# High parts of some weight panels moved 128 bytes on in their SBUF slots

## The chip, the cores and the metric

The kernel runs on one core of a Trainium2 chip. The metric is the device time of one execution in microseconds; three runs of the kernel before gave 839.09, 839.23 and 839.39 us (median 839.23).

## The reference

Two layers of a transformer on 256 tokens of width 1024, all in float32. Each layer has a mixer and a feed-forward part, both with a residual sum and a layer norm behind them:

```python
z = x @ w_in                                   # 1024 x 5904: latents, FoX q/k/v, DSA q/k/v, index, gates
o_mla = causal attention over keys/values made from a 128 wide latent (8 heads, 96 wide)
o_fox = causal attention with a cumulative log forget gate added to the scores (8 heads)
o_dsa = attention over the 64 keys picked by an index score (8 heads, shared key and value)
merged = sum_n sigmoid(gates_n + b_gate) * (o_n @ w_branch[n])
x = layernorm(ALPHA * x + merged @ w_out)
u = x @ w_up                                   # 1024 x 5632: gate and value halves
y = (gelu(conv3(u[..., :2816])) * u[..., 2816:]) @ w_down
x = layernorm(ALPHA * x + y)
```

## The kernel before, in words

**Products.** TensorE multiplies in a rounded float32 form. To keep the precision, every operand is split into a high part (rounded copy) and a low part (the rest), and a product is three matmuls, written by `product` (L670 to L674): `a_hi` with `b_hi` (L672), `a_hi` with `b_lo` (L673), `a_lo` with `b_hi` (L674). In each, `a` is the stationary operand (loaded into the array by LDWEIGHTS, 128 columns) and `b` the moving one. In a row's `ps<-X,Y` the first name is the moving operand and the second the stationary one. While one matmul streams its moving operand, the LDWEIGHTS of the next matmul reads that one's stationary tile.

**Panels.** The weights come in 72 panels a layer (`NP`), up to 2048 floats a partition. SP loads a panel into a slot of `raw` (six slots); ACT's `split_hi` (L1146) writes the high part into a slot of `w_hi` (four slots); DVE's `split_lo` (L1491) writes the low part into `w_lo`, which lies on the very addresses of `raw`. TensorE waits for `weights_lo` of the panel and frees it with `panel_used`. The order of all engines' work is written out by hand.

**Two ways to use a panel.** "By feature": the weight tile is stationary, the transposed activations are moving (FoX queries and keys, gates, branch panels, and 19 of the 22 up panels in `ffn_up`, L1012). "By token": the activations are stationary and the weights moving. By token go the two first panels (`A_AT`, 432 columns), the two panels of FoX values (`FV_AT`, 512 columns), the first three up panels (`up_by_token`, L1025, 256 columns), the out panels and the down panels (512 columns). FoX values are 24 matmuls a panel, 96 in the two layers. The up panels by token are done for token half 0 first (72 matmuls), then for half 1 (72), so 288 in the two layers; inside the third one of half 0 stand transposes of the second half of `x` (`turn_x`, L719), which wait for DVE's norm, and the first panel of half 1 waits for `x_lo_ready` before its fifth tile.

**Where the tiles lie.** The tensors lie one behind another in each partition, in the order of the code, so each address follows from the sizes. `raw` and `w_lo` start at byte 2,176, `w_hi` at 51,328, `xt_hi` and `xt_lo` (transposed `x`) at 92,480 and 100,672, `ot_hi` (attention outputs) at 116,032, `ot_hi_last` at 193,856, `mg_hi` at 173,184, `ht_hi` (hidden) at 133,248. Small unused tensors (`PADS`) set these. Taken modulo 256: `raw`, `w_lo`, `w_hi`, `mg` and `ht` have 128; `xt`, `ot` and `ot_last` have 64. `merged` has 192. Slots of 2048 floats are 8,192 bytes, which is 0 modulo 256. The first two panels of layer 0 are already moved by `FIRST_SHIFT` = 32 floats (128 bytes) in all three tensors (L437, L443, L449); in layer 1 they have places of their own (`early_hi` and `early_lo`, both 0 modulo 512), with tiles 1,728 bytes apart.

Of the kernel before, what the change touches and what calls it, by code (L numbers as in the profile page):

```python
# [19 lines left out]
F32R = mybir.dt.float32r  # L20
# [6 lines left out]
P = 128  # L27
# [30 lines left out]


PANEL = 2048  # L60

A_AT, FV_AT, FQ_AT, UQ_AT, FK_AT, KEYS_AT, IQ_AT, UKV_AT, SQ_AT = 0, 2, 4, 6, 7, 9, 10, 11, 12
GATE_AT = 14
# [2 lines left out]
UP_AT = OUT_AT + 4  # L66
# [1 line left out]
DOWN_K = [4, 3, 3, 3, 3, 3, 3]  # L68
NP = DOWN_AT + 2 * len(DOWN_K)
NGATED = 4  # L70
PADS = (48, 24, 112, 48, 208)
NHI, NLO = 4, 6
EARLY = (A_AT, A_AT + 1)
FIRST_SHIFT = 32
SKEWED = 4
UP_BY_TOKEN = 3

# [2 lines left out]
TAKEN = -3.3e38  # L80
# [57 lines left out]
def build_program(nc, x, positions, w_in, b_gate, b_forget, q_norm, kv_norm, w_uq, w_ukv, w_branch, w_out,  # L138
                  ln1_g, ln1_b, w_up, conv_w, conv_b, w_down, ln2_g, ln2_b, out):
    ctx = ExitStack()  # L140
    with ctx:
        def sb(name, shape, dt=F32):
            return ctx.enter_context(nc.sbuf_tensor(name, shape, dt))
# [123 lines left out]
        def slot_of(l, p, n):  # L267

            return n + p - A_AT if is_early(l, p) else turn_of(l, p) % n
# [13 lines left out]
        with ExitStack() as over:  # L283
            raw = over.enter_context(nc.sbuf_tensor("raw", [P, NLO, PANEL], F32))
        w_lo = sb("w_lo", [P, NLO, PANEL], F32R)
        w_hi = sb("w_hi", [P, NHI, PANEL], F32R)
        x_tok = sb("x_tok", [P, NT, DM])
        sb("beside_x", [P, PADS[0]])
        xt_hi = sb("xt_hi", [P, KD, T], F32R)
# [14 lines left out]
        eps = sb("eps", [P, 2])  # L304
        sb("beside_outputs", [P, PADS[1]])
        with ExitStack() as over:
# [14 lines left out]
        with ExitStack() as att:  # L321
            sa = sized(att)
            z1 = sa("z1", [P, NT, ZW])
            gates_early = sa("gates_early", [P, SLOTS // 2, T])
            with ExitStack() as over:
                so = sized(over)
                rel_first = so("rel_first", [P, 4, T])
                rel_second = so("rel_second", [P, 4, 2 * T])
            gates_late = sa("gates_late", [P, SLOTS // 2, T])
            with ExitStack() as over:  # L330
                so = sized(over)
                merged = so("merged", [P, KD, T])
                gated = so("gated", [P, NGATED, T])
            fq_t = sa("fq_t", [P, 4, T])
            fk_t = sa("fk_t", [P, 4, T])
            fv = sa("fv", [P, NT, H * HD])
            sa("beside_merged", [P, PADS[2]])
            with ExitStack() as over:
                so = sized(over)
                mg_hi = so("mg_hi", [P, KD, T], F32R)  # L340
                mg_lo = so("mg_lo", [P, KD, T], F32R)
            qm_t = sa("qm_t", [P, H, T])
            km_t = sa("km_t", [P, H, T])
            v_tok = sa("v_tok", [P, NT, H * HD])
            sa("beside_last", [P, PADS[3]])
            with ExitStack() as over:
                so = sized(over)
                ot_hi_last = so("ot_hi_last", [P, 4, T], F32R)
                ot_lo_last = so("ot_lo_last", [P, 4, T], F32R)
            decay = sa("decay", [P, H, T])  # L350
            decay_first = sa("decay_first", [P, H, P])
            sq_t = sa("sq_t", [P, 4, T])
            sk_t = sa("sk_t", [P, T])
            with ExitStack() as over:
                so = sized(over)
                pts_odd = so("pts_odd", [P, 2, 3 * P])
            ik_t = sa("ik_t", [P, T])
            iq_t = sa("iq_t", [P, 2, T])
            rsum = sa("rsum", [P, 2, 2, NT])
            rinv = sa("rinv", [P, 2, 2, NT])  # L360
            least = sa("least", [P, 2, 2, NT])
            small = sa("small", [P, 16])
            fx = sa("fx", [P, NT, H])
            fe = sa("fe", [P, NT, H])
            fl = sa("fl", [P, NT, H])
            cum = sa("cum", [P, NT, H])
            with ExitStack() as lat:
                sl = sized(lat)
                sl("beside_latents", [P, 24])
                c_hi = sl("c_hi", [P, 3, T], F32R)  # L370
                c_lo = sl("c_lo", [P, 3, T], F32R)
                with ExitStack() as over:
                    so = sized(over)
                    c_f = so("c_f", [P, 3, T])
                    cn = so("cn", [P, NT, QR + KVR])
                rot = sl("rot", [P, 4, NT, H, HALF])
                q_rope = sl("q_rope", [P, NT, H * ROPE])
                krot = sl("krot", [P, 4, NT, HALF])
                kr = sl("kr", [P, NT, ROPE])
            with ExitStack() as heads:  # L380
                sh = sized(heads)
                prob = sh("prob", [P, 2, 2, 3 * P])
                pts_even = sh("pts_even", [P, 2, 3 * P])
                ix = sh("ix", [P, 3 * P])
                ixw = sh("ixw", [P, 3 * P])
                top8 = sh("top8", [P, 8])
                selm = sh("selm", [P, 3 * P])

        with ExitStack() as ffn:
            sf = sized(ffn)  # L390
            sf("beside_hidden", [P, PADS[4]])
            ht_hi = sf("ht_hi", [P, FT, T], F32R)
# [30 lines left out]
        SPAN = (slice(0, P), slice(P, 3 * P))  # L423
# [9 lines left out]
        def panel_raw(l, p):  # L433

            if is_early(l, p):
                return early_raw[:, p - A_AT, :]
            return raw[:, slot_of(l, p, NLO), FIRST_SHIFT if p in EARLY else 0:]  # L437

        def panel_lo(l, p):

            if is_early(l, p):
                return early_lo[:, p - A_AT, :]
            return w_lo[:, slot_of(l, p, NLO), FIRST_SHIFT if p in EARLY else 0:]  # L443

        def panel_hi(l, p):

            if is_early(l, p):
                return early_hi[:, p - A_AT, :]
            return w_hi[:, slot_of(l, p, NHI), FIRST_SHIFT if p in EARLY else 0:]  # L449

        def turned(i):

# [159 lines left out]
        def panel_extents(p):  # L612
# [9 lines left out]
            if p >= DOWN_AT:  # L622
                return [(P, slice(0, 512 * DOWN_K[(p - DOWN_AT) % len(DOWN_K)]))]
            return [(P, slice(0, PANEL))]

# [43 lines left out]
        def _(pe):  # L669
# [387 lines left out]
            for l in range(DEPTH):  # L1057
# [71 lines left out]
                for c in range(2):  # L1129
                    for g in range(ng if c == 0 else ng - SKEWED):  # L1130
                        k0, nk = sum(DOWN_K[:g]), DOWN_K[g]
# [3 lines left out]
                        for t, ins in by_token(l, DOWN_AT + ng * c + g, k0, nk, 512, (ht_hi, ht_lo), B_R[c],  # L1135
                                               g == 0, g == ng - 1):
                            if g == ng - 1 and t == 0:
                                ins.then_inc(s_residual_product, 1)
                        ins.then_inc(s_panel_used, 1)
                one_token_first(l, [(NP - ng + g, 1, sum(DOWN_K[:g]), DOWN_K[g], False, g == ng - 1)  # L1140
                                    for g in range(ng - SKEWED, ng)], (ht_hi, ht_lo), SKEWED - 1 if l < DEPTH - 1 else None)

# [347 lines left out]
        def _(dve):  # L1490
# [106 lines left out]
            def take_eight(l, n):  # L1597

                t = n // (TOPK // 8)
                if n % (TOPK // 8) == 0:  # L1600
                    dve.wait_ge(s_index_masked, at("index_masked", l, t + 1))
                dve.drain()
                dve.max(top8[:], ixw[:, SPAN[t]])
                dve.drain()
                dve.match_replace(ixw[:, SPAN[t]], top8[:], ixw[:, SPAN[t]], TAKEN)

            def selection(l):

# [410 lines left out]
```

## Time and profile before

| | us |
|---|---|
| median of three runs | 839.23 |
| the profiled execution, whole | 840.46 |
| its span, first to last instruction | 838.7 |
| TensorE matmuls busy | 826.2 (99% of the span) |
| VectorE busy | 605.2 (72%) |
| ScalarE busy | 464.1 (55%) |

The profile is one execution of the program. Matmuls are pipelined: one lasts longer than the distance to the start of the next, and their ends are modelled, so what a matmul costs is read from the distance between starts, and its recorded duration is only a sign of it.

### The profile page before, as it was taken

What the parts mean: (1) busy time and instruction counts of PE and PEld (TensorE: products, weight loads), DVE (VectorE), ACT (ScalarE), POOL (GpSimd) and SP (SyncE); (2) the same over time, 40 slices, a digit from 0 to 9 for tenths busy, and PEclk for the clock granted to TensorE, in tenths of its full rate; (3) what the DMA queues carried; (4) which work ended last, traced back from release to release, by engine and by line L of the source; (5) the groups of instructions that cost most, each with busy time, mean ns of one, the idle gap of its engine ahead of it and who ended that gap; (6) DMA issues with size and microseconds to landing.
All of it is one profiled execution on the core that took longest, in us unless ns stands there. A gap on an engine that the chain in (4) does not pass through costs nothing.

```text
span 838.7 us, 15687 instructions
## 1 busy us (share of the span) xinstructions
PE 826.2 (99%) x6326; PEld 770.9 (92%) x6326; DVE 605.2 (72%) x1076; ACT 464.1 (55%) x701; POOL 113.8 (14%) x133
## 2 busy tenths in 40 slices
PE   7999999999999999999999999999999999999996
PEld 6899999999899999988889998998998999999885
DVE  5675788987786877765676568888797687777554
ACT  5675866663456655543447576756545475555440
POOL 1503910006300000000000067000180000000000
PEclk9999999999999999999999999999999999999999
DMA  9959643344579766475847694443467767764731
GB/s 307 240 131 280 192 137 117 136 152 151 165 189 240 197 193 184 160 244 175 267 114 190 127 333 118 145 131 122 151 185 198 190 190 195 200 189 151 250 115 50
DMA packets 190265, 150.98 MB, mean 180 GB/s; under 512 B 32653, under 2 KB 164337, under 8 KB 189937
## 3 DMA queue, kind: packets, MB, share of 16 engines
q1 hardware_dynamic: 181120, 143.09, 57.9%
q10 hardware_dynamic: 9072, 6.90, 3.0%
q8 instruction: 50, 0.82, 0.4%
q14 instruction: 23, 0.18, 0.1%
HBM read 148.63 MB, written 1.06 MB: 178 GB/s over the span
## 4 chain that ended last, share of the span: by engine, by line
PE 92%; DMA 2%; DVE 2%; POOLq 1%; SPq 1%; ACT 1%; ACTq 1%; POOL 1%; issue 0%; DVEq 0%
PE ps L672 28%; PE ps L674 27%; PE ps L673 27%; PE ps L955 3%; PE ps L986 2%; PE ps L967 2%; POOLq L1989 1%; DMA decay<-decay_rows 1%; DMA raw<-w_in 1%; PE ps L730 1%; DVE w_lo L1499 1%; ACTq L1203 0%; ACT w_hi L1154 0%; PE ps L1052 0%; POOL rel_first L1986 0%
## 5 line engine op out<-in xcount | busy, mean ns | idle before, releaser
L1499 DVE TENSOR_TENSOR w_lo<-raw,w_hi 128x2048 fp32r<-128x2048 f32 (+2 forms) x140 | 303.2, 2167 | 111.5 <-ACT w_hi L1154 111.4
L672 PE MATMUL ps<-xt_hi,w_hi 128*128 128x256 f32 x1232 | 344.9, 280 | 0.0
L673 PE MATMUL ps<-xt_lo,w_hi 128*128 128x256 f32 x1232 | 340.6, 276 | 0.0
L674 PE MATMUL ps<-xt_hi,w_lo 128*128 128x256 f32 x1232 | 340.5, 276 | 0.0
L1154 ACT ACTIVATE w_hi<-raw 128x2048 fp32r<-128x2048 f32 (+3 forms) x142 | 253.0, 1786 | 77.9 <-PE ps L674 71.0
L672 PEld LDWEIGHTS ps<-xt_hi,w_hi 128*128 128x128 f32 x1232 | 231.3, 188 | 3.3 <-issue 2.0
L673 PEld LDWEIGHTS ps<-xt_lo,w_hi 128*128 128x128 f32 x1232 | 231.7, 188 | 0.0
L674 PEld LDWEIGHTS ps<-xt_hi,w_lo 128*128 128x128 f32 x1232 | 231.3, 188 | 0.0
L672 PE MATMUL ps<-w_hi,ht_hi 128*128 128x512 f32 x176 | 68.6, 390 | 0.0
L674 PE MATMUL ps<-w_hi,ht_lo 128*128 128x512 f32 x176 | 68.5, 389 | 0.0
L673 PE MATMUL ps<-w_lo,ht_hi 128*128 128x512 f32 x176 | 68.5, 389 | 0.0
L1275 ACT ACTIVATE cv<-ps,vec_t 128x256 f32<-128x256 f32 x44 | 20.8, 474 | 81.4 <-PE ps L674 77.8
L1999 POOL TENSOR_TENSOR merged<-merged,gated 128x256 f32<-128x256 f32 x32 | 40.2, 1282 | 177.3 <-DVE gated L1681 177.3
L1238 ACT ACTIVATE prob<-prob,least 128x128 f32<-128x128 f32 x96 | 42.8, 448 | 17.3 <-DVE least L1639 17.3
L672 PE MATMUL ps<-w_hi,xt_hi 128*128 128x256 f32 (+2 forms) x144 | 46.4, 322 | 0.9 <-DVE xt_lo L1506 0.7
L674 PE MATMUL ps<-w_hi,xt_lo 128*128 128x256 f32 (+2 forms) x144 | 45.1, 313 | 0.0
L673 PE MATMUL ps<-w_lo,xt_hi 128*128 128x256 f32 (+2 forms) x144 | 45.0, 312 | 0.0
L1971 POOL COPY km_t<-km_t 32x1792 f32<-32x1792 f32 x2 | 3.3, 1673 | 294.2 <-ACT km_t L1231 294.2
L1729 DVE SCALAR_TENSOR_TENSOR cv<-ps,vec_t,cv 128x255 f32<-128x255 f32 x44 | 21.2, 483 | 30.2 <-ACT cv L1275 29.9
L674 PEld LDWEIGHTS ps<-w_hi,ht_lo 128*128 128x128 f32 x176 | 33.0, 188 | 6.9
L672 PEld LDWEIGHTS ps<-w_hi,ht_hi 128*128 128x128 f32 x176 | 33.0, 188 | 6.8
L673 PEld LDWEIGHTS ps<-w_lo,ht_hi 128*128 128x128 f32 x176 | 33.0, 188 | 6.7
(252 smaller groups left out, 1276.1 us busy)
## 6 DMA issues: line engine op xcount, KB each, us to landing
raw<-ffn_w_up SPq DMA_DIRECT2D x88, 512.0 KB, 5.2
raw<-w_in SPq DMA_DIRECT2D x84, 512.0 KB, 5.5
raw<-ffn_w_down SPq DMA_DIRECT2D x32, 512.0 KB, 4.0
raw<-w_branch SPq DMA_DIRECT2D x24, 512.0 KB, 4.4
raw<-w_out SPq DMA_DIRECT2D x16, 512.0 KB, 4.6
raw<-ffn_w_down SPq DMA_DIRECT2D x24, 256.0 KB, 3.0
decay<-decay_rows ACTq DMA_DIRECT2D x2, 1024.0 KB, 8.6
ln_g<-ln_g ACTq DMA_DIRECT2D x4, 512.0 KB, 3.5
```

The costliest lines, as they stand in the source:

```text
L672: pe.matmul(dst, a_hi, b_hi, start=first, stop=False)
L673: pe.matmul(dst, a_hi, b_lo, start=False, stop=False)
L674: return pe.matmul(dst, a_lo, b_hi, start=False, stop=last)
L955: ins = pe.matmul(ps[:, B_S[a], SPAN[t]], q[:, P * t:P * t + P], k[:, 0:P * (t + 1)], start=True, stop=True)
L967: ins = pe.transpose(ps[:, B_PT[a], P * c:P * c + P], prob[:, i % 2, a, P * c:P * c + P], ident[:])
L986: ins = pe.matmul(dst[HD * a:HD * a + HD, P * c:T], v, turned(i)[:, a, cols], start=c == 0, stop=c == 1)
L1154: ins = act.activation(panel_hi(l, p)[0:n, cols], panel_raw(l, p)[0:n, cols], ACT.Copy)
L1238: ins = act.activation(p, p, ACT.Exp, scale=-1.0, bias=least[:, i % 2, a, t:t + 1], accum_out=rsum[:, i % 2, a, t:t + 1])
L1275: act.activation(cv[:, buf, :], ps[:, B_UP[f % len(B_UP)], 0:T], ACT.Copy, scale=column(vec_t, V_CW + 2 * FT, f)).then_inc(s_conv_first_ta ...
L1499: ins = dve.tensor_tensor(low, panel_raw(l, p)[0:n, cols], panel_hi(l, p)[0:n, cols].bitcast(F32), ALU.subtract)
L1729: dve.scalar_tensor_tensor(cv[:, buf, 1:T], ps[:, B_UP[f % len(B_UP)], 0:T - 1], column(vec_t, V_CW + FT, f), cv[:, buf, 1:T], ALU.mult, A ...
L1999: pool.tensor_tensor(merged[:, u % KD, :], merged[:, u % KD, :], gated[:, u % NGATED, :], ALU.add).then_inc(s_merged_added, 1)
```

## The change

The high parts of seven panels (the two first ones, as before, and now also the two of FoX values and the three up panels by token) begin 32 floats (128 bytes) into their slot of `w_hi`. Their raw and low parts stay where they were, except for the two first ones, which were moved already. For this the slots of `w_hi` become 64 floats (256 bytes) longer, `SLOT` = 2112. To find the room, a pad in front of `mg_hi` shrinks from 112 to 48 floats, and the small tile `top8` (top eight index scores) takes the place of another pad instead of room of its own.

```diff
+SLOT = PANEL + 64
-PADS = (48, 24, 112, 48, 208)
+PADS = (48, 24, 48, 48, 208)
+SHIFTED = (A_AT, A_AT + 1, FV_AT, FV_AT + 1, UP_AT, UP_AT + 1, UP_AT + 2)
-        w_hi = sb("w_hi", [P, NHI, PANEL], F32R)
+        w_hi = sb("w_hi", [P, NHI, SLOT], F32R)
-            sa("beside_last", [P, PADS[3]])
+            top8 = sa("top8", [P, PADS[3]])
-                top8 = sh("top8", [P, 8])
-            return w_hi[:, slot_of(l, p, NHI), FIRST_SHIFT if p in EARLY else 0:]
+            at0 = FIRST_SHIFT if p in SHIFTED else 0
+            return w_hi[:, slot_of(l, p, NHI), at0:at0 + PANEL]
-                dve.max(top8[:], ixw[:, SPAN[t]])
+                dve.max(top8[:, 0:8], ixw[:, SPAN[t]])
-                dve.match_replace(ixw[:, SPAN[t]], top8[:], ixw[:, SPAN[t]], TAKEN)
+                dve.match_replace(ixw[:, SPAN[t]], top8[:, 0:8], ixw[:, SPAN[t]], TAKEN)
```

No instruction is added or removed. Everything that lies behind `w_hi` moves by 1,024 bytes, what lies behind the shortened pad (`mg_hi` and on, within the attention part) by 768, and `selm` by 736.

## Rows read from the trace of the kernel before

**Rows 1.** The page, part 1: busy us (share of the span) xinstructions.
```profile
PE 826.2 (99%) x6326; PEld 770.9 (92%) x6326; DVE 605.2 (72%) x1076; ACT 464.1 (55%) x701; POOL 113.8 (14%) x133
```

**Rows 2.** The page, part 4: shares of the chain that ended last.
```profile
PE 92%; DMA 2%; DVE 2%; POOLq 1%; SPq 1%; ACT 1%; ACTq 1%; POOL 1%; issue 0%; DVEq 0%
```

**Rows 3.** Timeline (start us, duration us, instruction) of PE, a feature-wise up panel, layer 0.
```profile
278.54 0.28 PE L672 MATMUL ps<-xt_hi,w_hi 128*128 128x256 f32 x1
...
283.98 0.28 PE L672 MATMUL ps<-xt_hi,w_hi 128*128 128x256 f32 x1
```

**Rows 4.** Timeline of PE, up panels by token, layer 0, first half of tokens.
```profile
237.06 0.28 PE L672 MATMUL ps<-w_hi,xt_hi 128*128 128x256 f32 x1
...
244.01 0.28 PE L674 MATMUL ps<-w_hi,xt_lo 128*128 128x256 f32 x1
```

**Rows 5.** Timeline of PE, a down panel of three tiles, layer 0.
```profile
373.98 0.39 PE L673 MATMUL ps<-w_lo,ht_hi 128*128 128x512 f32 x1
...
378.06 0.39 PE L673 MATMUL ps<-w_lo,ht_hi 128*128 128x512 f32 x1
```

**Rows 6.** Timeline of PE, FoX value panels of layer 1, second half of tokens.
```profile
436.81 0.39 PE L672 MATMUL ps<-w_hi,xt_hi 128*128 128x512 f32 x1
...
442.08 0.40 PE L674 MATMUL ps<-w_hi,xt_lo 128*128 128x512 f32 x1
```

**Rows 7.** Groups by line, same stretch: xcount | busy us, mean ns.
```profile
L672 PE MATMUL ps<-w_hi,xt_hi 128*128 128x512 f32 x8 | 3.2, 394 | 0.0
L674 PE MATMUL ps<-w_hi,xt_lo 128*128 128x512 f32 x8 | 3.1, 393 | 0.0
L673 PE MATMUL ps<-w_lo,xt_hi 128*128 128x512 f32 x8 | 3.1, 388 | 0.0
```

**Rows 8.** Timeline of PE, first feature-wise panel (FoX queries) of layer 0.
```profile
31.94 0.28 PE L673 MATMUL ps<-xt_lo,w_hi 128*128 128x256 f32 x1
...
37.59 0.28 PE L673 MATMUL ps<-xt_lo,w_hi 128*128 128x256 f32 x1
```

**Rows 9.** Line L674: duration ns min/median/max, first and last start us.
```profile
L674 PE MATMUL ps<-xt_hi,w_lo x1232: 276/276/286, 32.1 to 771.2; 128*128 128x256 f32 x176
...
L674 PE MATMUL ps<-ot_hi_last,w_lo x64: 281/281/281, 202.9 to 625.1; 128*128 128x256 f32 x64
```

**Rows 10.** Timeline of PE, the two first panels of layer 1 (432 columns).
```profile
433.31 0.35 PE L672 MATMUL ps<-early_hi,xt_hi 128*128 128x432 f32 x1
...
433.90 0.35 PE L672 MATMUL ps<-early_hi,xt_hi 128*128 128x432 f32 x1
...
435.65 0.35 PE L672 MATMUL ps<-early_hi,xt_hi 128*128 128x432 f32 x1
...
436.24 0.35 PE L672 MATMUL ps<-early_hi,xt_hi 128*128 128x432 f32 x1
```

**Rows 11.** Timeline of PE around its two waits in the up panels by token.
```profile
244.32 0.66 PE L730 MATMUL ps<-ident,x_tok 128*128 128x128 f32 x4
...
248.25 0.39 PE L672 MATMUL ps<-w_hi,xt_hi 128*128 128x256 f32 x1
```

**Rows 12.** Timeline of DVE, what those two waits wait for.
```profile
243.51 0.75 DVE L1719 SCALAR_TENSOR_TENSOR x_tok<-res,rdev,ln_b 128x512 f32<-128x512 f32 x1
...
247.50 0.69 DVE L1506 TENSOR_TENSOR xt_lo<-ps,xt_hi 128x512 fp32r<-128x512 f32 x1 [1.15 <-ACT xt_hi L1161]
```

**Rows 13.** Timeline of DVE: the normed latents that PE takes after FoX values, layer 1.
```profile
441.20 0.94 DVE L1544 TENSOR_SCALAR cn<-z,small 128x192 f32<-128x192 f32 x4
```

**Rows 14.** Lines L1744, L1686, L1255, L1286: duration ns min/median/max, first and last start.
```profile
L1744 DVE TENSOR_TENSOR ht_lo<-hf,ht_hi x44: 417/419/429, 260.7 to 775.9; 128x256 fp32r<-128x256 f32 x44
...
L1686 DVE SCALAR_TENSOR_TENSOR mg_lo<-merged,mg_hi x16: 411/681/986, 209.2 to 629.4; 128x256 fp32r<-128x256 f32 x16
...
L1255 ACT ACTIVATE mg_hi<-merged x16: 400/419/420, 206.4 to 628.9; 128x256 fp32r<-128x256 f32 x16
...
L1286 ACT ACTIVATE ht_hi<-hf x44: 401/407/419, 260.2 to 775.5; 128x256 fp32r<-128x256 f32 x44
```

## The prediction

> **What bounds the kernel.** I read the page's busy shares first: TensorE is busy for 826.2 of 838.7 us [rows 1]. The chain of waits confirms it, with 92% of the span on PE [rows 2]. So time can only move where matmuls start closer together or further apart, or where TensorE waits. No instruction changes, so everything hangs on addresses, and I read the timeline for the distance between matmul starts, against the addresses that the front part lists.
>
> Call D the moving operand's address minus that of the stationary tile loaded beside it, modulo 256. I pick 256 because all the pads differ within it; what speaks for that period stands below.
>
> - D = 0 (down panels: `w` and `ht` both at 128): from 373.98 to 378.06 us are 18 matmuls of 512 columns, 226.7 ns each [rows 5].
> - D = 64 (up panels by token, `w` at 128 moving, `xt` at 64 stationary): the 60 matmuls from 237.06 to 244.01 make 59 distances of 117.8 ns [rows 4]. FoX values have the same D: 24 matmuls, 23 distances over 5.27 us, 229.1 ns each [rows 6]. By line, the two kinds that stream `w_hi` last 394 and 393 ns, the one that streams `w_lo` 388 [rows 7].
> - D = 192 (feature-wise panels, `xt` moving, `w` stationary): 48 matmuls from 278.54 to 283.98, 113.3 ns each [rows 3]. But the same D also has a dear price: the first FoX query panel of layer 0 takes 117.7 ns for each of its 48 (31.94 to 37.59) [rows 8]. By duration, 276 ns is the median of the 1232 feature-wise ones and 281 that of all 64 on `ot_hi_last`, which have D = 192 as well [rows 9].
>
> So a matmul of 256 columns has two prices, 113.3 and 117.8, 4.5 ns apart. At D = 64 I see only the dear one; at D = 192 mostly the cheap one, and in some runs of panels the dear one throughout. What picks the price at D = 192 no row tells me.
>
> **The change part by part.**
>
> *The shift.* `w_hi` of the seven panels goes from 128 to 0 modulo 256. For FoX values and the three up panels a matmul that streams `w_hi` (L672 and L674, two in three) then has D = 0 - 64 = 192; the one that streams `w_lo` (L673) keeps 64. Up panels: if L672 and L674 go to the cheap price, each gains 4.5 ns. The lower end is 0 (D = 192 at its dear price costs 117.7, what they cost now, so no row has a loss here); the upper end is that all three kinds get it, as each LDWEIGHTS shadows a neighbour. I take the two kinds in three: the row of FoX values already has the third apart from the others.
>
> Which of them are on the path? TensorE waits twice in these panels. At 244.32 it starts transposes 0.31 us after the last matmul before them (244.01) [rows 4, 11], where 0.12 is the usual distance; DVE's norm, 243.51 to 244.26, ends just before [rows 12]. DVE began that chain from the out product, so the 60 matmuls before it gain nothing: TensorE waits longer instead. The 12 behind it are on the path, since the next transposes follow them and ACT and DVE follow those. The next 12 are hidden again: the matmul behind them starts at 248.25, just after the end of DVE's `xt_lo` (247.50 to 248.19) [rows 11, 12]. The last 60 are on the path: nothing but TensorE stands between 248.25 and the feature-wise panels. So 72 of 144 a layer, 144 in both, of which 96 stream `w_hi`: 96 x 4.5 ns = 0.43 us (0 to 144 x 4.5 = 0.65).
>
> FoX values: 96 matmuls. Down panels show what 512 columns cost without the loss, 226.7 [rows 5], against 229.1 [rows 6]: 96 x 2.4 = 0.23 us, between 0 and, from the durations of 394 and 393 against 388, 64 x 5.5 = 0.35. In layer 1 TensorE goes from them to the transposes of the latents, at 442.08 + 0.23 = 442.31 [rows 6], and DVE has those ready at 441.20 + 0.94 = 442.14 [rows 13]. The cover is 0.17 us and the last 24 matmuls gain 24 x 2.4 = 0.06, so nothing is late next. In layer 0 the transposes wait for a copy that itself follows TensorE. All 96 count.
>
> *The splits.* ACT then writes `w_hi` at 128 bytes from its source modulo 256, and DVE reads `raw` and `w_hi` at such a distance; 10 panels. The nearest rows: DVE on `merged` (192) and `mg_hi` (128) has a minimum of 411 ns, on `hf` and `ht_hi` (both 128) 417; ACT has minima of 400 and 401 with and without an offset of 64 [rows 14]. The medians of 681 and 419 are in the stretch where GpSimd adds `merged`. I take 0. Were it 411 against 417 either way, 10 panels of eight times the length would move by 10 x 8 x 6 ns = 0.5 us of DVE time, which stands beside TensorE.
>
> *Longer slots, moved tensors.* A slot step of 8,448 bytes is 33 x 256: odd slots get 256 bytes more, all D stay. 1,024 and 768 are multiples of 256 too. Is 256 the whole period? The two first panels of layer 1 differ by 256 modulo 512. Their third tile (D = 64 in one, 320 modulo 512 in the other) takes 433.31 to 433.90 and 435.65 to 436.24: 0.59 us for three matmuls both times [rows 10]. I take 0. `selm` (736 bytes) and `top8` only meet DVE; 0.
>
> **The sum.** 0.43 + 0.23 = 0.66 us, so 840.46 - 0.66 = 839.80 for the profiled execution, which was 1.23 us above the median; on the scale of the runs 839.23 - 0.66 = **838.6 us**, 0.08% less. With the ends: 839.2 to 838.2.
>
> Differences under 0.2% (1.7 us) I call no change; this is about what a measurement of this kernel can tell.
>
> **A rule that speaks against it.** What the rows show first: matmuls of the same shape, back to back, differ by 4.5 ns with the addresses [rows 3, 4]. The Trainium skill (SBUF — State Buffer, "Who interferes with whom") says that TensorE has two independent read ports, one for the moving operand and one for LDWEIGHTS, and never waits on anyone. By that rule D has no price, and the sum would be 0. The trace doesn't agree with it fully, though it doesn't prove that the addresses are the cause.
>
> **Rivals.**
>
> 1. *Nothing moves.* The by-token order costs 117.8 for another reason (the order of reads, the `w_lo` matmul that holds its neighbours at the dear price), as D = 192 also has 117.7 [rows 8]. For it: a price seems to persist over whole panels. Against: FoX values, where just the kinds on `w_hi` are long [rows 7]. 839.2 us.
> 2. *More panels turn cheap.* The price may be handed on from one panel to the next. The queries and first keys of layer 0 (144 matmuls) run right behind FoX values; freed, they give 144 x 4.5 = 0.65 us more: 837.9. The branch matmuls on `ot_hi_last` (64 of each kind, 192 in both layers [rows 9]) would give 192 x 4.5 = 0.86 us more: 837.1. Against the second part: what stands before them keeps its D. With both, and 0.2 for `w_lo` on top, 836.9.
> 3. *Slower: the other up panels turn dear.* The 19 feature-wise up panels follow the moved ones, and they have the cheap price [rows 3]. If the new alternation of 192 and 64 hands them the dear price, 912 matmuls a layer cost 4.5 ns more, 4.1 us: 843 us with one layer, 847 with both. It decides at the first panel behind the up panels by token; from about 520 such matmuls (521 x 4.5 = 1.7 + 0.66 us) it is over the bound. Against: transposes with a gap lie between, and behind gaps this D nearly always ends cheap.
> 4. *Slower: 512 is the period.* Then odd slots have a D of their own; half of 3696 feature-wise matmuls dear is 1848 x 4.5 = 8.3 us: 847. Against it rows 10.
>
> **How the numbers follow.** Forecast as priced (838.2 to 839.0): 0.52. Rival 1: 0.18. Rival 2: 0.18, of which 0.12 under 837.6 (its second part included). Rival 3: 0.08. Rival 4: 0.04. Faster by over 0.2% (below 837.6): 0.12 from rival 2 and 0.04 for a gain on `w_lo` and on waits together with the first part of rival 2: 0.16. Slower: 0.12. Within: 0.72. The range of 8 in 10 is 837.2 to 839.9: it leaves out the far end of rival 2 and rivals 3 and 4.
>
> **What would show it.** In the trace after: L672 and L674 of the up panels by token last 276 instead of 280 ns, L673 stays; distances there average (2 x 113.3 + 117.8) / 3 = 114.8. In FoX values L672 and L674 last 388, distances 227. The wait before 244.3 grows by 60 x 3.0 = 0.2 us. Feature-wise panels and splits keep their durations, in odd slots too. The forecast fails if the by-token distances stay at 117.8, if a panel elsewhere changes its price, or if `split_lo` of the ten panels leaves 2.29 us.

## The result and the profile after

The changed kernel took 843.42 us (median of 20 executions, 839.49 to 847.72), the kernel before beside it 839.20 (838.78 to 839.88, one execution of 1389.82 set aside). The ratio is 1.0040, with an interval of 1.0030 to 1.0051: slower by 0.4%, where no change was forecast. A median hides the shape: six executions lie at 839.5 to 840.6, thirteen at 843.2 to 844.6 and one at 847.7. That is three levels, some 4 us apart. The profiled execution is one of the middle level (843.45 us, span 841.7). In the changed kernel `product` has the lines L674, L675 and L676.

The page, busy shares, and the shares of the chain [rows 1, 2]:
```profile
PE 829.5 (99%) x6326; PEld 774.1 (92%) x6326; DVE 605.5 (72%) x1076; ACT 464.4 (55%) x701; POOL 112.9 (13%) x133
```
```profile
PE 91%; POOL 3%; DVE 2%; issue 1%; DMA 1%; SPq 1%; ACT 1%; POOLq 0%; DVEq 0%
```
Only TensorE has moved, by 3.3 us in as many instructions: no engine has taken its place as the bound.

Timeline of PE in layer 0, the 18 feature-wise up panels behind the four transposes (start us, duration us, instruction), first and last of 864 matmuls, and the first down matmul:
```profile
261.03 0.60 PE L1054 MATMUL ps<-ident,u_tok 128*128 128x128 f32 x4
261.39 0.36 PE L674 MATMUL ps<-xt_hi,w_hi 128*128 128x256 f32 x1
261.59 0.28 PE L675 MATMUL ps<-xt_lo,w_hi 128*128 128x256 f32 x1
...
363.11 0.28 PE L676 MATMUL ps<-xt_hi,w_lo 128*128 128x256 f32 x1
363.23 0.39 PE L674 MATMUL ps<-w_hi,ht_hi 128*128 128x512 f32 x1
```
The same block in layer 1:
```profile
675.89 0.60 PE L1054 MATMUL ps<-ident,u_tok 128*128 128x128 f32 x4
676.24 0.37 PE L674 MATMUL ps<-xt_hi,w_hi 128*128 128x256 f32 x1
676.45 0.28 PE L675 MATMUL ps<-xt_lo,w_hi 128*128 128x256 f32 x1
...
774.15 0.28 PE L676 MATMUL ps<-xt_hi,w_lo 128*128 128x256 f32 x1
774.26 0.39 PE L674 MATMUL ps<-w_hi,ht_hi 128*128 128x512 f32 x1
```
Layer 0: 363.11 - 261.39 = 101.72 us over 863 distances, 117.9 ns each. Layer 1: 97.91, 113.5 each, as before [rows 3]. The same panels, at addresses that the change did not move against one another, cost 3.8 us more in one layer than in the other. Two such layers, one or none would make the three levels; of the changed kernel only the middle one was profiled. No single row shows it, each matmul lasts 0.28 us in both: one has to divide a stretch by its count.

Up by token, layer 0, first and last of 60 [rows 4]; the second half of the FoX values of layer 1, first and last of 24 [rows 6]; and the first panel of FoX queries of layer 0, first and last of 48 [rows 8]:
```profile
236.13 0.28 PE L674 MATMUL ps<-w_hi,xt_hi 128*128 128x256 f32 x1
...
243.09 0.28 PE L676 MATMUL ps<-w_hi,xt_lo 128*128 128x256 f32 x1
...
439.94 0.39 PE L674 MATMUL ps<-w_hi,xt_hi 128*128 128x512 f32 x1
...
445.25 0.40 PE L676 MATMUL ps<-w_hi,xt_lo 128*128 128x512 f32 x1
```
```profile
31.57 0.37 PE L674 MATMUL ps<-xt_hi,w_hi 128*128 128x256 f32 x1
...
36.99 0.28 PE L676 MATMUL ps<-xt_hi,w_lo 128*128 128x256 f32 x1
```
By token: 6.96 us over 59, 118.0 ns, no gain. FoX values: 5.31 over 23, 230.9, where 229.1 stood: dearer. FoX queries: 5.42 over 47, 115.3 with the long first distance of 0.20 us in it; behind that one the distance went from 117.8 to 113.4 in all 96 matmuls of the queries (0.4 us saved). In layer 1 the same panels went the other way.

Where the 3.0 us of span came from, from distances times counts: TensorE reaches the up panels by token 0.93 us earlier (236.13 against 237.06, of which the queries are 0.41 and the branch panels 0.37); then the first feature-wise panel of layer 0 costs 48 x 4.3 = 0.2 and the block 864 x 4.4 = 3.8. The down product starts 363.23 - 360.14 = 3.1 us later, and layer 1, where small terms of both signs cancel (queries and one gate panel +0.6, keys and branch -0.6), keeps it.

### The profile page after: what moved, and what is told of

It reads as the page before. It is cut to its first block, busy times and chain, and to the rows that moved or that the text cites. A ratio compares the mean times of both kernels' runs of the same rounds, so it can differ in the third digit from the quotient of the medians.

```text
span 841.7 us, 15687 instructions
## 1 busy us (share of the span) xinstructions
PE 829.5 (99%) x6326; PEld 774.1 (92%) x6326; DVE 605.5 (72%) x1076; ACT 464.4 (55%) x701; POOL 112.9 (13%) x133
## 4 chain that ended last, share of the span: by engine, by line
PE 91%; POOL 3%; DVE 2%; issue 1%; DMA 1%; SPq 1%; ACT 1%; POOLq 0%; DVEq 0%
PE ps L674 28%; PE ps L676 27%; PE ps L675 27%; POOL merged L2001 3%; PE ps L957 3%; PE ps L969 2%; PE ps L988 2%; DVE w_lo L1501 1%; DMA raw<-w_in 1%; ACT w_hi L1156 1%; PE ps L732 1%; PE ps L919 0%; PE ps L1054 0%; SPq L636 0%; DVE x_tok L1721 0%
## 5 line engine op out<-in xcount | busy, mean ns | idle before, releaser
L1501 DVE TENSOR_TENSOR w_lo<-raw,w_hi 128x2048 fp32r<-128x2048 f32 (+2 forms) x140 | 303.1, 2167 | 112.2 <-ACT w_hi L1156 111.8
L674 PE MATMUL ps<-xt_hi,w_hi 128*128 128x256 f32 x1232 | 346.4, 281 | 0.0
L675 PE MATMUL ps<-xt_lo,w_hi 128*128 128x256 f32 x1232 | 342.1, 278 | 0.0
L676 PE MATMUL ps<-xt_hi,w_lo 128*128 128x256 f32 x1232 | 342.1, 278 | 0.0
L1156 ACT ACTIVATE w_hi<-raw 128x2048 fp32r<-128x2048 f32 (+3 forms) x142 | 252.7, 1784 | 77.8 <-PE ps L676 71.3
L674 PEld LDWEIGHTS ps<-xt_hi,w_hi 128*128 128x128 f32 x1232 | 232.6, 189 | 3.3 <-issue 2.0
L675 PEld LDWEIGHTS ps<-xt_lo,w_hi 128*128 128x128 f32 x1232 | 231.6, 188 | 0.0
L676 PEld LDWEIGHTS ps<-xt_hi,w_lo 128*128 128x128 f32 x1232 | 231.5, 188 | 0.0
L674 PE MATMUL ps<-w_hi,ht_hi 128*128 128x512 f32 x176 | 68.6, 390 | 0.0
L676 PE MATMUL ps<-w_hi,ht_lo 128*128 128x512 f32 x176 | 68.5, 389 | 0.0
L675 PE MATMUL ps<-w_lo,ht_hi 128*128 128x512 f32 x176 | 68.5, 389 | 0.0
L674 PE MATMUL ps<-w_hi,xt_hi 128*128 128x256 f32 (+2 forms) x144 | 46.5, 323 | 0.4 <-DVE w_lo L1501 0.4
L675 PE MATMUL ps<-w_lo,xt_hi 128*128 128x256 f32 (+2 forms) x144 | 45.2, 314 | 0.0
L676 PE MATMUL ps<-w_hi,xt_lo 128*128 128x256 f32 (+2 forms) x144 | 45.2, 314 | 0.0
L676 PEld LDWEIGHTS ps<-w_hi,ht_lo 128*128 128x128 f32 x176 | 33.0, 188 | 6.9
L674 PEld LDWEIGHTS ps<-w_hi,ht_hi 128*128 128x128 f32 x176 | 33.0, 188 | 6.8
L675 PEld LDWEIGHTS ps<-w_lo,ht_hi 128*128 128x128 f32 x176 | 33.0, 188 | 6.8
```

The source lines that it names most:

```text
L674: pe.matmul(dst, a_hi, b_hi, start=first, stop=False)
L675: pe.matmul(dst, a_hi, b_lo, start=False, stop=False)
L676: return pe.matmul(dst, a_lo, b_hi, start=False, stop=last)
L1156: ins = act.activation(panel_hi(l, p)[0:n, cols], panel_raw(l, p)[0:n, cols], ACT.Copy)
L1501: ins = dve.tensor_tensor(low, panel_raw(l, p)[0:n, cols], panel_hi(l, p)[0:n, cols].bitcast(F32), ALU.subtract)
```

## The experiments

Below, "the block" is the 864 matmuls of feature-wise up panels 4 to 21 of a layer, "the first panel" is panel 3 ahead of it, "cheap" is about 113.3 ns and "dear" about 117.8 ns between starts. Experiments whose ratios are given together ran beside the same executions of the kernel before. A mean distance leaves out the pauses at waits; where it is taken over a whole stretch from first to last start, the first long distance is in it.

### Which part of the change does it

The kernel before took 839.62 us beside these. `e1_slots` has the longer slots and the moved small tensors, but shifts only the two first panels; `e1_fv` also FoX values; `e1_up` also the up panels, without FoX values.
```diff
-SHIFTED = (A_AT, A_AT + 1, FV_AT, FV_AT + 1, UP_AT, UP_AT + 1, UP_AT + 2)
+SHIFTED = (A_AT, A_AT + 1)                                  # e1_slots
+SHIFTED = (A_AT, A_AT + 1, FV_AT, FV_AT + 1)                # e1_fv
+SHIFTED = (A_AT, A_AT + 1, UP_AT, UP_AT + 1, UP_AT + 2)     # e1_up
```


> Longer slots, the shorter pad and the moved top8, but no further panel shifted. Theory 1 and 3: 839.2 us, all up panels at 113.3 ns. Theory 2 (odd slots or moved tensors): levels of 839.5, 843.5 and 847.7 as after.

> Only the two FoX value panels are shifted. Theory 1: the up panels stay at 113.3 ns; the queries of layer 0 may be cheap and FoX values cost 231 instead of 229 ns (both as in the profile after), so 838.5 to 839.5 us. Theory 2: 839.5 to 847.7, several levels. Theory 3: 843.5 and 847.7 appear here.

> Only the three up panels by token are shifted (the FoX value panels lie as before). Theory 1 (the by-token up panels hand their price on to the 19 up panels behind them: the alternation of D = 192 and 64 ends in the dear phase): some executions at about 839.5, 843.5 and 847.7 us, as after; in the profile a layer's 912 matmuls at 117.8 ns in at least one execution. Theory 2 (the longer slots or moved tensors do it): the same times, but then also without any shift. Theory 3 (the FoX value shift does it): 839 us throughout.

Measured: slots 839.77 us (1.0004, 0.9995 to 1.0012), FoX values 840.04 (1.0005, 0.9996 to 1.0014), up panels 842.69 (1.0038, 1.0019 to 1.0057). The first two have eleven executions each, and none at a level: the highest are 841.68 and 842.00, and nothing recorded says why these two are 2 us above their median. The third has the levels: six of twelve at 839.6 to 841.5, four at 843.9 to 844.7, two at 847.2 and 848.2. So the loss belongs to the shift of the up panels by token. In its profile the block is cheap in layer 0 and dear in layer 1, the mirror of the changed kernel:
```profile
672.45 0.60 PE L1054 MATMUL ps<-ident,u_tok 128*128 128x128 f32 x4
672.81 0.36 PE L674 MATMUL ps<-xt_hi,w_hi 128*128 128x256 f32 x1
673.01 0.28 PE L675 MATMUL ps<-xt_lo,w_hi 128*128 128x256 f32 x1
...
774.53 0.28 PE L676 MATMUL ps<-xt_hi,w_lo 128*128 128x256 f32 x1
```
In layer 1 the block takes 774.53 - 672.81 = 101.72 us over 863 distances, 117.9 ns each. The FoX value matmuls of `e1_fv` take 231.1 ns in both layers: their shift costs by itself.

These runs also show something of the up panels by token, which the prediction took as dear by their address. In layer 1 of `e1_slots`, where these panels are not shifted, the last 60 of them (token half 1) run cheap:
```profile
659.28 0.38 PE L674 MATMUL ps<-w_hi,xt_hi 128*128 128x256 f32 x1
...
666.07 0.28 PE L676 MATMUL ps<-w_hi,xt_lo 128*128 128x256 f32 x1
```
6.79 us over 59, 115.1 ns; without the first long distance 113.3. Layer 0 of `e1_fv` does the same, and the other layer of each stays at 117.8. So an address difference of 64 has both prices too.

Two more divide the up panels: `e2_first` shifts panels 0 and 1 of the three, `e2_last` panel 2, the last before the feature-wise ones.
```diff
+SHIFTED = (A_AT, A_AT + 1, UP_AT, UP_AT + 1)                # e2_first
+SHIFTED = (A_AT, A_AT + 1, UP_AT + 2)                       # e2_last
```


> The first and second up panel are shifted, the third is not. Theory 1: 839.6 us throughout, f = 3 at 113.6 ns in both layers. Rival 1b: levels of 839.6, 843.8 and 848. If the third panel carries on what the second leaves, a mixture.

> Of the up panels only the third, the last one by token before the feature-wise ones, is shifted. Theory 1 (the last by-token panel hands its price on): levels of 839.6, 843.8 and 848 us as in the run with all three, and the first feature-wise up panel (f = 3) at 117.8 ns in both layers. Rival 1b (the first shifted panel starts it): 839.6 us, f = 3 at 113.6.

Measured, beside 839.48 us: 839.93 us (1.0006, 0.9997 to 1.0014) and 839.90 (1.0004, 0.9995 to 1.0012), no execution of eleven each above 841.0. Each theory expected levels from one of the two, and neither has them. With panels 0 and 1 the first panel is cheap in both layers; with panel 2 it is dear in layer 1, cheap in layer 0; with all three shifted it is dear in the eight profiled layers where eight transposes stand ahead of it (two layers each of the changed kernel, `e1_up` and the two kernels with breaks below), and cheap in both layers of `e3_nobreak` below, where twelve do. So the last shifted panel can turn the next one; a dear block I have seen only with all three shifted.

### Is it the address difference?

Five variants of the kernel before, with nothing but pads changed, so that `xt` lies elsewhere modulo 256.
```diff
-PADS = (48, 24, 112, 48, 208)
+PADS = (64, 8, 112, 48, 208)       # e1_xt128: tiles at 128
+PADS = (16, 56, 112, 48, 208)      # e2_xt192: at 192
+PADS = (32, 40, 112, 48, 208)      # e2_xt0: at 0
+PADS = (56, 16, 112, 48, 208)      # e3_xt96: at 96
+PADS = (40, 32, 112, 48, 208)      # e3_xt32: at 32
```


> The kernel before, with xt_hi and xt_lo 64 bytes further on (128 modulo 256): D = 0 for feature-wise and by-token panels of 1024 wide inputs. Theory A (the conflict depends on D and D = 0 is free, as the down panels show at 226.7): all of these at 113.3 ns, by token too, no second price: about 144 x 4.5 + 96 x 2.4 + 340 x 4.5 ns = 2.4 us less, 836.8 us. Theory B (at 256 columns both streams meet in one bank for the whole matmul when D = 0): 117.8 ns or more for all 4300 matmuls, 858 us or more. Theory C (addresses have no price, only the order and phase of instructions): 839.2 us.

> The kernel before with xt_hi and xt_lo at 192 modulo 256: D becomes 64 for feature-wise and 192 for all three kinds by token. If D alone sets the price: by token 113.3 to 117.8 ns, feature-wise 117.8 for some 3000 matmuls, 13 us more, 852 us. If the order matters and not D: 839.2.

> The kernel before with xt at 0 modulo 256: D = 128 in both orders. The 432 column panels of the kernel before have about 196.5 ns at D = 128 against 192 to 193 at 0, so I expect a price between 113.3 and 119.9; at 117.8 it is 852 us, at 113.3 without a second price 837.

> The kernel before with its stationary tiles of turned states moved to byte 96 of the period of 256 (difference 224 feature-wise, 32 by token; was 192 and 64). Theory (the price goes by the difference, and 0 gives 120.0, 192 gives 113.3 or 117.8): 224 lies between them, 113.3 to 120.0 ns for the 256-column matmuls feature-wise, so 839 to 856 us; a steady cheap price would give 839, a steady one of 117.8 some 850. Rival (only steps of 64 bytes count, 224 behaves as 192 and 32 as 0): 839 to 845 us.

> The same with the tiles at byte 32 (difference 160 feature-wise, 96 by token). Theory: between the prices of 128 and 192, that is 113.3 to 118.7 ns feature-wise, 839 to 856 us. Rival (steps of 64 bytes count, 160 behaves as 128 and 96 as 64): as the tiles at byte 0, about 856 us.

Measured (mean distance in ns between starts; D is the prediction's, moving minus stationary modulo 256; where two values stand, layer 0 and 1, or two groups of panels):

| `xt` at | D by feature | 256 columns | D by token | 256 columns | 512 columns | us, ratio |
|---|---|---|---|---|---|---|
| 64 (before) | 192 | 113.4, some 117.8 | 64 | 117.8 | 229.1, 229.5 | 839.28 to 839.62 |
| 192 | 64 | 117.8, some 113.4 | 192 | 117.3, 115.7 | 233.3, 233.1 | 852.94, 1.0161 |
| 32 | 160 | 117.3, 118.8 | 96 | 119.8 | 233.3 | 854.66, 1.0184 |
| 96 | 224 | 118.3 | 32 | 117.3, 116.9 | 233.1, 233.3 | 856.32, 1.0205 |
| 0 | 128 | 118.7 | 128 | 120.0 | 232.2, 233.2 | 858.07, 1.0223 |
| 128 | 0 | 120.0 | 0 | 119.8 | 226.7, 228.9 | 862.05, 1.0266 |

Addresses alone are worth 22 us here, and the place of before is the best of the six. The down panels, whose tiles did not move, kept 226.7 to 226.9 ns throughout. For 256 columns the difference 0 is among the dearest (119.8 to 120.0, with 128), for 512 it is the cheapest; 192 has the cheap price for 256 and is among the dear ones for 512 (all but 0 and 64 lie at 232.2 to 233.5). Of the expectations, those hold that priced by the difference (theory B of `e1_xt128`, 852 us for `e2_xt192`, 118.7 ns feature-wise in `e2_xt0`, a price between its neighbours for 224 and, but for the groups at 118.8, for 160); those fall that took 0 as free, the addresses as without a price, or only steps of 64 as counting.

The difference doesn't settle everything: at 0, with all three kinds alike, the FoX values of layer 1 keep 228.9. And by token at 192, again with all three kinds alike, the first 60 of `e2_xt192` stay dear in both layers; layer 0:
```profile
239.45 0.28 PE L672 MATMUL ps<-w_hi,xt_hi 128*128 128x256 f32 x1
...
246.40 0.28 PE L674 MATMUL ps<-w_hi,xt_lo 128*128 128x256 f32 x1
```
6.95 us over 59, 117.8 ns. Of the last 60, those of layer 0 have 117.8 and those of layer 1 113.6. Groups by line, `e1_xt128`, layer 0, feature-wise (xcount | busy us, mean ns):
```profile
L674 PE MATMUL ps<-xt_hi,w_lo 128*128 128x256 f32 x209 | 59.1, 283 | 0.0
L672 PE MATMUL ps<-xt_hi,w_hi 128*128 128x256 f32 x209 | 59.1, 283 | 0.0
L674 PEld LDWEIGHTS ps<-xt_hi,w_lo 128*128 128x128 f32 x209 | 40.1, 192 | 0.0
L672 PEld LDWEIGHTS ps<-xt_hi,w_hi 128*128 128x128 f32 x209 | 40.1, 192 | 0.0
L673 PEld LDWEIGHTS ps<-xt_lo,w_hi 128*128 128x128 f32 x209 | 40.1, 192 | 0.0
```
Here each of these LDWEIGHTS lasts 192 ns. The same groups of the changed kernel, in its dear block and in its cheap one:
```profile
L674 PEld LDWEIGHTS ps<-xt_hi,w_hi 128*128 128x128 f32 x283 | 54.3, 192 | 0.0
L675 PEld LDWEIGHTS ps<-xt_lo,w_hi 128*128 128x128 f32 x284 | 53.3, 188 | 0.0
L676 PEld LDWEIGHTS ps<-xt_hi,w_lo 128*128 128x128 f32 x284 | 53.3, 188 | 0.0
...
L674 PEld LDWEIGHTS ps<-xt_hi,w_hi 128*128 128x128 f32 x283 | 53.1, 188 | 0.0
L675 PEld LDWEIGHTS ps<-xt_lo,w_hi 128*128 128x128 f32 x283 | 53.1, 188 | 0.0
L676 PEld LDWEIGHTS ps<-xt_hi,w_lo 128*128 128x128 f32 x282 | 52.9, 188 | 0.0
```
In a dear stretch at D = 192 exactly one load of three is long, the same line for 864 matmuls; in a cheap one none is. At this difference the state of a stretch can be read from that row. By token at a difference of 64 it can't: the kernel before has 117.8 ns there with all loads at 187 to 188.

### Is the state set at the entry and held?

`e3_nobreak` moves the last four transposes ahead of the first panel, so that all 19 panels run without a break. `e3_reset` adds breaks to the changed kernel ahead of panels 5, 6, 7 and 8, `e4_reset1` one ahead of panel 5.
```diff
+                turn_up(l, 2)                                # e3_nobreak
                 ffn_up(l, 3)
-                turn_up(l, 2)
...
+                if f in (5, 6, 7, 8):                        # e3_reset; e4_reset1: f == 5
+                    for _ in range(2):
+                        pe.transpose(ps[:, B_UP[f % len(B_UP)], 0:P], ident[:], ident[:])
```


> The changed kernel with the last turn of the hidden state moved ahead of the first feature-wise up panel, so that the transposes no longer stand between that panel and the 18 behind it. Theory (price set at the entry and held): all 19 panels of a layer have one price, 912 matmuls at either 113.3 or 117.8 ns, so the levels lie at about 839.5, 843.6 and 847.7 us, with no mixed case of a first panel that is dear and a block that is cheap; and as the first panel was dear in every profile with a shifted panel, 847.7 in most. Rival (what makes the block dear is the entry at the second panel alone, behind the four transposes): the break is gone and with it the cause, and all executions lie at 839.5 to 840.5 us.

> The changed kernel with two extra identity transposes ahead of each of the feature-wise up panels 5 to 8 of both layers (16 in all, output never read). Theory (the price of a stretch of panels is set where the matmuls begin again after other work, and held until the next such place): a block that enters at 117.8 ns gets four more entries and turns to 113.3 at one of them, so dear blocks last at most some 48 to 240 matmuls, 1.1 us instead of 3.9; executions at 843 us and above vanish or become rare, and the median falls to 840 to 842 us, the extra transposes costing up to 16 x 0.11 us and up to 8 x 0.1 us of re-entry. Rival (the layer's price is settled by something else than the entry: addresses, the buffer in turn, the partner load): the blocks stay at 117.8, the median is 844 to 846 us and the three levels of the changed kernel stay, 1 to 2 us higher.

> The changed kernel with two extra identity transposes ahead of the feature-wise up panel 5 alone, in both layers (their output is never read). With four such breaks (ahead of panels 5 to 8) the executions lay together at 842.0 to 843.0 us. Theory (a panel block takes its price at the entry and holds it; a block that came in dear gets another entry and turns cheap): the levels of the changed kernel at 843 to 845 us vanish, and with two breaks in place of eight the median is 840.0 to 840.8 us. Rival (an entry is a draw with no regard to what went before, so one more entry changes nothing but where the draw is made): the levels stay with the same shares, median 843 to 844 us, and the profile shows blocks of 816 matmuls at 117.8 ns.

`e3_nobreak` (before: 839.28): seven executions at 838.7 to 839.4 and five at 843.3 to 843.8, median 839.38, ratio 1.0021 (1.0006 to 1.0036). None is at 847, and the share that the theory expected was wrong: most executions had no dear layer. The times can't tell a dear layer of 912 from one of 864, and only one execution, of the lower level, was profiled. That profile has all 912 cheap in both layers (end of the stretch of layer 1):
```profile
666.74 0.37 PE L674 MATMUL ps<-xt_hi,w_hi 128*128 128x256 f32 x1
...
770.09 0.28 PE L676 MATMUL ps<-xt_hi,w_lo 128*128 128x256 f32 x1
```
103.35 us over 911, 113.4 each. The first panel, dear in every profile of the changed kernel's order, is cheap here. The rival (the cause is the second entry alone) falls as well, since five executions are still on the upper level.

`e3_reset`: 842.65 us (five executions, 841.97 to 843.0), ratio 1.0039 (1.0027 to 1.0051). None of the five shows the cost of a dear block, but the breaks eat the gain and the median misses the 840 to 842 us of the theory: in both layers the prices by panel are dear, cheap, cheap, dear, cheap, and the remaining 672 cheap. The 96 dear ones a layer cost 2 x 96 x 4.5 = 0.9 us, so by the times the eight breaks cost 842.65 - 839.5 - 0.9 = 2.3, some 0.28 each (an estimate). The trace gives 0.26: 257 ns from the last start of a panel to the first of the next in place of 114, and 47 distances of 115.7 in place of 113.3 behind it. Panel 6 shows that a break is no repair. It is entered from a cheap panel and is dear in both layers (47 distances of 119.5):
```profile
272.85 0.28 PE L676 MATMUL ps<-xt_hi,w_lo 128*128 128x256 f32 x1
272.97 0.38 PE L1021 MATMUL ps<-ident 128*128 128x128 f32 x2
273.10 0.36 PE L674 MATMUL ps<-xt_hi,w_hi 128*128 128x256 f32 x1
273.30 0.28 PE L675 MATMUL ps<-xt_lo,w_hi 128*128 128x256 f32 x1
```

`e4_reset1` (before: 839.09): three executions at 840.0 to 841.0, three at 843.6 to 844.4, median 842.31, ratio 1.0043 (1.0028 to 1.0057). The theory falls: one more entry doesn't remove the levels. The rival is right in that, but its blocks of 816 dear matmuls were not seen, since the one profile is of the lower level, 840.00 us, and has both blocks cheap behind the break. There layer 1 enters dear twice (panels 3 and 4) and leaves it at the break:
```profile
672.35 0.36 PE L674 MATMUL ps<-xt_hi,w_hi 128*128 128x256 f32 x1
672.55 0.28 PE L675 MATMUL ps<-xt_lo,w_hi 128*128 128x256 f32 x1
...
678.09 0.38 PE L1021 MATMUL ps<-ident 128*128 128x128 f32 x2
678.22 0.36 PE L674 MATMUL ps<-xt_hi,w_hi 128*128 128x256 f32 x1
...
770.70 0.28 PE L676 MATMUL ps<-xt_hi,w_lo 128*128 128x256 f32 x1
```
From 678.22: 92.48 us over 815 distances, 113.5.

What all profiles together show is that the entry isn't a plain draw. The long load of the stretch ahead goes with what follows. Loads of the first panel in the changed kernel, layer 0 and then layer 1 (groups by line):
```profile
L676 PEld LDWEIGHTS ps<-xt_hi,w_lo 128*128 128x128 f32 x12 | 2.3, 192 | 0.0
L674 PEld LDWEIGHTS ps<-xt_hi,w_hi 128*128 128x128 f32 x12 | 2.3, 188 | 0.0
...
L674 PEld LDWEIGHTS ps<-xt_hi,w_hi 128*128 128x128 f32 x12 | 2.3, 192 | 0.0
```
Where L676's load was the long one (layer 0 here, layer 1 of `e1_up`, layer 1 of `e4_reset1`: three cases) the panels behind the next break came in dear; where it was L674's (layer 1 here, layer 0 of `e1_up` and `e4_reset1`, layer 1 of `e2_last`, both of `e3_reset`, and the three dear panels ahead of a two-transpose break: nine cases) they came in cheap. So it looks as if something is carried through the transposes; this is a regularity of twelve cases, and no experiment set the long load on purpose. What decides which load is the long one stays open. The same program gives three levels, so it isn't the addresses alone.

### FoX values, by themselves

`e4_fv0` shifts the high parts of the FoX value panels alone, by 48 floats (192 bytes, D = 0). `e5_fv0both` and `e5_fv192both` move high and low parts of the first layer's panels together, by 48 and by 32 floats.
```diff
-            at0 = FIRST_SHIFT if p in SHIFTED else 0
+            at0 = FIRST_SHIFT if p in SHIFTED else 48 if p in (FV_AT, FV_AT + 1) else 0      # e4_fv0
...
+GAPS = (2, 3)                                                # e5: 64 floats behind slots 2 and 3 of raw, w_lo, w_hi
+            at0 += FIRST_SHIFT if p in EARLY else 48 if (l, p) in ((0, FV_AT), (0, FV_AT + 1)) else 0
```


> The longer slots with the FoX value panels alone moved, by 192 bytes instead of 128, so that their difference to the stationary tiles is 0 instead of 192; up panels unmoved. Theory (a 512-column matmul is dear by its difference: 226.7 to 226.8 ns at 0, 229.2 at 64, 231.1 at 192): the FoX value matmuls take 226.8 ns in both layers, 96 x 2.4 = 0.23 us under the kernel before and 0.4 under the values at 192; median 839.0 to 839.6 us, no execution at 843. Rival (in the second layer something else sets it, as in the run with the tiles at 128, whose second layer kept 229.1 ns at difference 0): 226.8 in the first layer and about 229 in the second, half the gain.

> The kernel before with the FoX value panels of the first layer alone lying 192 bytes further on, this time their low parts too (gaps of 256 bytes behind slots 2 and 3 of both areas make room; everything behind them lies where it does in the changed kernel); the second layer's panels are unmoved. Theory (what made the panels at difference 0 dear, 231.9 ns, is that their high parts alone were moved and every third matmul still reads a low part at 64): the first layer's 48 matmuls take 226.8 ns, the second layer's 229.2 to 229.8; median 839.0 to 839.8 us. Rival (the difference is not what prices these matmuls): 229 to 232 ns in the first layer again.

> The same with 128 bytes in place of 192, so that high and low parts of the first layer's FoX value panels both have the difference 192 that the changed kernel gives to the high parts alone. Theory (price by the difference of all three kinds): 233.3 ns as with the tiles at 192, above the 231.1 of the changed kernel. Rival (moving high and low parts apart is what costs): 229.2 ns, as before.

`e4_fv0`: 839.64 us (1.0006, 0.9998 to 1.0015), and 231.9 and 231.6 ns: theory and rival fall. With the low parts moved too (before: 839.29): 226.7 ns at D = 0 and 233.5 at D = 192 in the first layer; both theories hold, to 0.2 ns. Groups by line in the second half of these panels, `e5_fv0both` (lines L681 to L683), then `e5_fv192both`:
```profile
L683 PE MATMUL ps<-w_hi,xt_lo 128*128 128x512 f32 x8 | 3.1, 390 | 0.0
L681 PE MATMUL ps<-w_hi,xt_hi 128*128 128x512 f32 x8 | 3.1, 389 | 0.0
L682 PE MATMUL ps<-w_lo,xt_hi 128*128 128x512 f32 x8 | 3.1, 389 | 0.0
```
```profile
L683 PE MATMUL ps<-w_hi,xt_lo 128*128 128x512 f32 x8 | 3.2, 396 | 0.0
L682 PE MATMUL ps<-w_lo,xt_hi 128*128 128x512 f32 x8 | 3.2, 396 | 0.0
L681 PE MATMUL ps<-w_hi,xt_hi 128*128 128x512 f32 x7 | 2.8, 395 | 0.0
```
In the first layer the price goes by the difference where all three kinds of a product share it, and an uneven shift has a price of its own: 0 with 64 costs 231.9, more than either alone (226.7, 229.1). In the second layer it doesn't hold as well (228.9 at D = 0 in `e1_xt128`), and why stays open. `e5_fv0both` ran at 839.10 against 839.29 (0.9998, 0.9988 to 1.0007), with a gain by count of 48 x 2.4 = 0.1 us. `e5_fv192both` has one execution, 838.96, though its count says 48 x 4.4 = 0.2 us more. Neither can be told from the kernel before by its time; both are ahead of the changed kernel.

## Why the prediction was wrong

The forecast was 838.6 us, with 837.2 to 839.9 as its range; measured were 843.42. What failed above all is a term that the prediction put at nothing: it took the feature-wise up panels to keep their price, and in the profile 864 of them went from 113.3 to 117.8 ns, 3.8 us. The two terms of its sum failed too, for less. The six executions of 20 at 839.5 to 840.6 show what is left without that: still no gain.

- *"So time can only move where matmuls start closer together or further apart."* Right: in the traces it is distances that moved, and the 3.0 us of span come out of them.
- *D, modulo 256, as the price.* Right in kind, and not the whole: moving `xt` alone moved the distances of all panels that read it, but 64 and 192 have two prices each at 256 columns. The steps of 64 that I had seen are not all there is, since 32 and 96 have prices of their own. `e1_xt128` took 22.4 us more than the kernel before. The rule that I had set against it, that of the Trainium skill (SBUF — State Buffer, "Who interferes with whom"), by which TensorE's two read ports are independent, would have made the two equal; the measurement decides. Which part of the reading makes the price, no run shows.
- *"If L672 and L674 go to the cheap price, each gains 4.5 ns": the first failed step, 0.43 us.* By token the distances stayed at 117.8 ns on average in all 288 matmuls. They are now uneven: some 20 a layer at 114 or 115 ns and about as many at 120 to 122. D = 192 has two prices, and I took the cheap one of the feature-wise order for this one. The mixture with 64 isn't needed to explain it: `e2_xt192` has all three kinds at 192 and is still dear in three of its four stretches of 60, while `e1_slots` and `e1_fv` have a cheap stretch at 64. So it is rival 1 that came true for these panels, in that something besides D decides between the two prices; what, stays open. The bound of 0 held it.
- *"Down panels show what 512 columns cost without the loss": the second failed step, 0.23 us.* I carried the order of prices from 256 columns (192 cheap) to 512, although the only 226.7 that I had belonged to D = 0. For 512 columns 192 is among the dear ones, 233.5 in `e5_fv192both`. With two kinds of three moved it was 231.1, a loss of 96 x 1.9 = 0.2 us in place of a gain of 0.23. My lower bound was 0, so the sign was outside the bounds.
- *Rival 3, "slower: the other up panels turn dear": dismissed at 0.08, and it decided.* Its levels ("843 us with one layer, 847 with both") are those measured, and `e1_up` shows its cause, the shift of the up panels by token. Its place is right by half: the first panel turned, but it holds 48 matmuls, and the 864 behind the four transposes were decided once more there (dear in layer 0, cheap in layer 1), 3.8 us in place of 4.1. That the new alternation of 192 and 64 is what hands on the price was not tested: no run shifts the low parts of these panels too. What I held against it, "transposes with a gap lie between, and behind gaps this D nearly always ends cheap", was a count of outcomes in one execution of another program. The shift acts through the transposes: with eight of them ahead the first panel was dear in eight of eight profiled layers, and the block, by the levels of the 20 executions, in 15 of the changed kernel's 40 layers.
- *Rival 2, "more panels turn cheap".* It came true in part (FoX queries of layer 0, 0.4 us, and 96 of the 168 branch matmuls a layer that were dear), but it isn't caused by the shift: the queries are cheap in `e2_last` too, whose FoX values lie as before, and in `e1_slots`, with no new shift, the dear branch matmuls, 168 a layer, went from 117.8 to 113.5. These short stretches change price from edit to edit.
- *The splits, and 256 as the period of the slots.* Right as far as the times show: DVE's split has 303.1 us after against 303.2, ACT's 252.7 against 253.0, and in `e1_slots` the longer slots alone left the time as it was (1.0004).
- *The waits.* Right in place, but with no gain by token there was nothing for them to swallow.

## What to carry to other kernels

Where TensorE is the bound and its matmuls are short, the address of the moving operand against the stationary one can be worth per cents (2.7% between the best and the worst place here): sweep it with a pad, all parts of a product together, and read the distance between starts in each group of equal matmuls. Price a case only from rows of the same width and the same mixture; a row of another width can have the other sign. If a state is seen to hold for hundreds of matmuls, what stands ahead of a long stretch is part of its price: multiply the difference by the longest stretch first, ask for several executions and look at their levels rather than their median.

## What the runs showed of the hardware

- One program has several lasting prices at the same addresses: 113.3 or 117.8 ns for a matmul of 256 columns, for 864 of them without a change. Feature-wise at a difference of 192, one LDWEIGHTS of three lasts 192 ns in the dear state and the others 188; at a difference of 0 all three last 192 and the distance is 120.0.
- An interruption of the stretch by two transposes costs 0.26 us by the trace, an estimated 0.28 by the times, with its re-entry, and the new stretch begins with a distance of 200 to 207 ns.
- With one pair of tensors at its best and at its worst place the kernel takes 839.62 and 862.05 us, 2.7% apart, with no instruction changed.
